# A float32 two-block transformer kernel: the split parts of each feed-forward are placed 32 to 96 bytes further on in SBUF

## The chip, the cores and the metric

The kernel runs on one core of one Trainium2 chip. The metric is the device time of one execution in microseconds (us), lower is better. Three runs of the kernel before took 1274.98, 1275.31 and 1278.06 us; their median is 1275.31 us.

## The reference, cut to what matters

256 tokens of width 1024 go through one block (feed-forward, mixer, feed-forward) and a second, modulated block (mixer, feed-forward). All of it is float32. The part that the change touches is the feed-forward, which comes three times; the third has a small convolution over tokens between the up projection and the product:

```python
D_MODEL, SEQ, D_FF = 1024, 256, 2816
def swiglu(x, w_gate, w_up, w_down):
    return (jax.nn.silu(x @ w_gate) * (x @ w_up)) @ w_down
```

## The kernel before, in words

**Tiles and order.** All weights come from DRAM as one stream of tiles of 128 x 1024 float32 (512 KB) in the order in which they are used. SyncE issues one DMA per tile into a ring of six places (`ring`); the DMA of tile t waits until TensorE has used tile t - 6. Every feed-forward k (0, 1, 2) takes 66 tiles: 22 gate, 22 up, 22 down, in the order down f - 2, gate f, up f.

**The split products.** TensorE multiplies in the type float32r. To keep the precision of float32, each operand is split: the upper part is a copy rounded to float32r, the lower part is the value less the upper part. A product is then three matmuls (`split_product`, L606 to L611):

```python
pe.matmul(out, w_hi[:, cols_], x_hi, start=start, stop=False, **kw)
pe.matmul(out, w_hi[:, cols_], x_lo, start=False, stop=False, **kw)
return pe.matmul(out, w_lo[:, cols_], x_hi, start=False, stop=stop, **kw)
```

Each matmul has a weight load of its own (128 x 128), which runs while the matmul before it still streams its moving operand (128 x 256, the 256 tokens). A tile has 8 chunks of 128 columns, so it makes 24 matmuls, and a feed-forward makes 66 x 24 = 1584: 44 gate and up tiles with 1056 matmuls (`gate_up`, L670, and `gate_up_first`, L688), and 22 down tiles with 528 (`down`, L699). In the gate and up products the moving operand is `u_hi` or `u_lo` (the split input, 8 chunks of 256), in the down products `hidden_hi` or `hidden_lo` (2 chunks of 256, by parity of f). The weights come from `ring_hi` and `ring_lo`.

**Who makes the parts.** ScalarE copies each arrived tile into `ring_hi` (L1429) and each `hidden` into `hidden_hi` (L1435). VectorE subtracts for `ring_lo` (L2074) and `hidden_lo` (L2080); of the tiles from the ninth on, every third `ring_lo` is made by GpSimd instead (L2794). The split inputs `u_hi` and `u_lo` are made once per feed-forward by ScalarE (L1416 and L1997) and VectorE (L2086 and L2092). Between them VectorE takes products (L2143, L2148; in the third feed-forward the convolution, L2160) and, in the first two, adds up the modulation of the second block (`condition`, L2105) in the three places `cond_sums`, which TensorE reads later (L743). All this goes beside TensorE; semaphores count tiles.

**Where things lie.** SBUF is laid out by hand, counted in float32 elements per partition from one start (`regions`, L175). Of these places, each begins 0 or 16 elements past a multiple of 32 elements, which is 0 or 64 bytes past a multiple of 128 bytes:

| name | used for | first element | bytes past a multiple of 128 |
|---|---|---|---|
| `own_parts` (the ring) | lower weights outside the feed-forwards | 0 | 0 |
| `u_parts` | mixer inputs | 8192 | 0 |
| `scratch_parts` | mixer inputs | 16688 | 64 |
| `parts` | all split parts of the feed-forwards; upper weights in the mixers | 20784 | 64 |
| `late_parts` | mixer inputs | 47920 | 64 |
| `branch_parts`, `branch_uppers` | branch inputs and upper weights | 41280, 35136 | 0, 0 |
| `single_upper`, number 18, 19, 20 | upper weights | 47424, 43328, 44352 | 0 |

Inside `parts` lie `ring_hi`, `ring_lo`, `u_hi`, `u_lo`, `hidden_hi` and `hidden_lo` at elements 0, 6144, 12288, 14336, 16384 and 16896 (`PARTS`, L210). Those, and every chunk of 128, 256 or 1024 elements in them, are whole multiples of 128 bytes apart. The same split products are also used in the mixers (`split_cols`, L588), with the operands of the table above.

## Time and profile before

| what | value |
|---|---|
| median of three runs | 1275.31 us (1274.98 to 1278.06) |
| profiled execution, first to last instruction | 1275.3 us |
| mean granted TensorE clock | 0.978 |
| TensorE matmuls, busy | 1215.8 us (95%), 9052 records |
| VectorE / ScalarE / GpSimd, busy | 837.7 / 632.1 / 534.4 us |
| feed-forward matmuls, three groups of 1584 | L609, L610, L611, operands all in `parts` |
| DMA | 207.03 MB, mean 162 GB/s |

The profiled execution's own time is that of its span, 1275.3 us, and is the same as the median of the runs. Matmul records overlap: one is listed with 0.28 us from its start to its end, but the next begins long before that end. What a matmul costs in a stream is the distance from one start to the next. In a view by stretches, a stretch whose ends are put just behind the start of one matmul and of a later one counts the matmuls that start in it and two or three that were still under way when it began; the notes to the rows say which.

### The profile page before, as it was taken

The numbers are of one execution on the slowest core, as the hardware profiler recorded it, in microseconds if no ns is written. First come the engines' busy times: TensorE is split into PE (matmuls) and PEld (weight loads), VectorE is DVE, ScalarE is ACT, GpSimd is POOL, SyncE is SP. The second block draws the span as 40 slices with busy tenths as digits, with TensorE's granted clock in tenths as the row PEclk, the third lists the DMA queues.
The fourth block names the chain that finished last, engine by engine and source line by source line (L and its number), as shares of the span: only waits on it lengthen the run. The fifth ranks groups of instructions, "written<-read, shape, count | busy, mean of one in ns | idle before, by whom it ended". The sixth has DMA issues, their size and how long they took to land.

```text
span 1275.3 us, 24245 instructions
## 1 busy us (share of the span) xinstructions
PE 1215.8 (95%) x9052; PEld 1137.3 (89%) x9052; DVE 837.7 (66%) x1146; ACT 632.1 (50%) x1008; POOL 534.4 (42%) x283
## 2 busy tenths in 40 slices
PE   6999998998999999999999999998899898999998
PEld 6999998976888999999999888977677798999998
DVE  6888875865964577776555843688737685655555
ACT  5444445616651554444435545566417535555553
POOL 0354336632451534334535644478430473232331
PEclk9999998999999999999989999999999998999999
DMA  8677863433333457777504323233212254555553
GB/s 318 234 262 283 281 216 104 149 116 117 116 100 118 163 199 248 279 278 266 181 32 149 125 90 133 84 100 99 83 67 100 83 165 133 185 181 183 186 182 105
DMA packets 58095, 207.03 MB, mean 162 GB/s; under 512 B 6576, under 2 KB 8240, under 8 KB 57776
## 3 DMA queue, kind: packets, MB, share of 16 engines
q1 hardware_dynamic: 49824, 177.23, 40.6%
q0 software_dynamic: 6912, 25.17, 5.4%
q10 hardware_dynamic: 1296, 3.74, 0.8%
q8 instruction: 45, 0.74, 0.2%
q14 instruction: 18, 0.15, 0.0%
HBM read 205.07 MB, written 1.05 MB: 162 GB/s over the span
## 4 chain that ended last, share of the span: by engine, by line
PE 79%; DVE 8%; ACT 4%; issue 4%; POOL 3%; DMA 1%; DVEq 0%; SPq 0%; POOLq 0%; ACTq 0%
PE psum L609 22%; PE psum L610 21%; PE psum L611 21%; PE psum L949 2%; POOL own_parts L2786 2%; PE psum L620 1%; POOL high L2869 1%; PE psum L622 1%; PE psum L621 1%; DMA low<-stream 1%; PE psum L743 1%; DVE parts L2074 1%; PE psum L897 1%; PE psum L663 1%; PE psum L634 1%
## 5 line engine op out<-in xcount | busy, mean ns | idle before, releaser
L609 PE MATMUL psum<-parts 128*128 128x256 f32 x1584 | 452.1, 285 | 17.3 <-DVE parts L2074 9.9
L610 PE MATMUL psum<-parts 128*128 128x256 f32 x1584 | 450.7, 285 | 0.0
L611 PE MATMUL psum<-parts 128*128 128x256 f32 x1584 | 450.6, 284 | 0.0
L609 PEld LDWEIGHTS psum<-parts 128*128 128x128 f32 x1584 | 306.8, 194 | 18.5 <-issue 15.7
L2794 POOL TENSOR_TENSOR parts<-low,parts 128x1024 fp32r<-128x1024 f32 x60 | 158.4, 2640 | 362.4 <-ACT parts L1429 362.4
L610 PEld LDWEIGHTS psum<-parts 128*128 128x128 f32 x1584 | 306.9, 194 | 0.0
L611 PEld LDWEIGHTS psum<-parts 128*128 128x128 f32 x1584 | 306.6, 194 | 0.0
L1429 ACT ACTIVATE parts<-low 128x1024 fp32r<-128x1024 f32 x198 | 207.9, 1056 | 177.8 <-DMA low<-stream 177.0
L2786 POOL TENSOR_TENSOR own_parts<-low,parts 128x1024 fp32r<-128x1024 f32 x76 | 188.0, 2487 | 197.3 <-ACT parts L1498 197.1
L2074 DVE TENSOR_TENSOR parts<-low,parts 128x1024 fp32r<-128x1024 f32 x138 | 164.8, 1218 | 23.3 <-ACT parts L1429 22.0
L611 PE MATMUL psum<-scratch_parts,own_parts 128*128 128x256 f32 (+1 forms) x496 | 150.2, 303 | 0.0
L2786 POOL TENSOR_TENSOR own_parts<-low,single_upper 128x1024 fp32r<-128x1024 f32 x31 | 77.3, 2500 | 73.3 <-ACT single_upper L1498 70.6
L609 PE MATMUL psum<-u_parts,parts 128*128 128x256 f32 x344 | 100.1, 291 | 5.9 <-DVE late_parts L2214 3.1
L611 PE MATMUL psum<-u_parts,own_parts 128*128 128x256 f32 x360 | 101.8, 283 | 0.0
L611 PEld LDWEIGHTS psum<-scratch_parts,own_parts 128*128 128x128 f32 x496 | 96.3, 194 | 3.6
L610 PE MATMUL psum<-late_parts,parts 128*128 128x256 f32 x344 | 97.5, 284 | 0.0
L1498 ACT ACTIVATE parts<-low 128x1024 fp32r<-128x1024 f32 x76 | 79.3, 1050 | 14.3 <-DMA low<-stream 14.2
L609 PE MATMUL psum<-scratch_parts,single_upper 128*128 128x256 f32 (+1 forms) x256 | 79.5, 310 | 6.8 <-POOL own_parts L2786 5.6
L2080 DVE TENSOR_TENSOR parts<-low,parts 128x256 fp32r<-128x256 f32 x66 | 61.2, 927 | 32.0 <-ACT parts L1435 32.0
L2105 DVE SCALAR_TENSOR_TENSOR high<-high,low 128x1024 f32<-128x1024 f32 x64 | 79.0, 1273 | 0.0
L609 PE MATMUL psum<-scratch_parts,parts 128*128 128x256 f32 (+1 forms) x240 | 75.8, 316 | 0.9 <-DVE high L2432 0.6
L609 PEld LDWEIGHTS psum<-u_parts,parts 128*128 128x128 f32 x344 | 66.5, 193 | 11.2 <-issue 7.8
(355 smaller groups left out, 2198.2 us busy)
## 6 DMA issues: line engine op xcount, KB each, us to landing
low<-stream SPq DMA_DIRECT2D x334, 512.0 KB, 3.5
high<-conditioning POOLq DMA_DIRECT2D x48, 512.0 KB, 5.1
high<-wuq ACTq DMA_DIRECT2D x1, 1152.0 KB, 11.0
low<-x SPq DMA_DIRECT2D x4, 256.0 KB, 5.8
high<-ctx ACTq DMA_DIRECT2D x1, 1024.0 KB, 5.7
out<-low SPq DMA_DIRECT2D x8, 128.0 KB, 1.8
low<-cst ACTq DMA_DIRECT2D x1, 850.5 KB, 5.4
low<-vec ACTq DMA_DIRECT2D x1, 157.5 KB, 5.8
```

What stands on the lines that cost most here:

```text
L609: pe.matmul(out, w_hi[:, cols_], x_hi, start=start, stop=False, **kw)
L610: pe.matmul(out, w_hi[:, cols_], x_lo, start=False, stop=False, **kw)
L611: return pe.matmul(out, w_lo[:, cols_], x_hi, start=False, stop=stop, **kw)
L620: pe.matmul(out, hi(k, n), w_hi[:, cols_], start=k == 0, stop=False)
L949: mm = pe.matmul(bank(name)[:, s * T:(s + 1) * T], w[:, (n % 2 * 4 + k) * P:(n % 2 * 4 + k + 1) * P], o[:, k, :], start=k == 0, stop=k == 3)
L1429: act.activation(ring_hi[:, j % RING, :], ring[:, t % RING, :], ACT.Copy)\
L1498: act.activation(weight_place(t), ring[:, t % RING, :], ACT.Copy)\
L2074: dve.tensor_tensor(ring_lo[:, j % RING, :], ring[:, t % RING, :], ring_hi[:, j % RING, :], ALU.subtract).then_inc(S("lower_ready"), 1)
L2080: dve.tensor_tensor(hidden_lo[:, par, :], hidden[:, par, :], hidden_hi[:, par, :], ALU.subtract).then_inc(S("hidden_split"), 1)
L2105: dve.scalar_tensor_tensor(out=acc_, in0=cond_places[g], scalar=small[:, bass.ds(i * 2 + who, 1)], in1=acc_, op0=ALU.mult, op1=ALU.add).th ...
L2786: pool.tensor_tensor(tile_lo[:, t % RING, :], ring[:, t % RING, :], weight_place(t), ALU.subtract).then_inc(S("weights_split"), 1)
L2794: pool.tensor_tensor(ring_lo[:, j % RING, :], ring[:, t % RING, :], ring_hi[:, j % RING, :], ALU.subtract).then_inc(S("lower_ready_2"), 1)
```

## The change

Each of the five regions behind `ring_hi` gets 32 more elements (128 bytes) of room, and a feed-forward reads and writes its parts at a start of its own inside these regions. `PART_STARTS` lists, for each of the three feed-forwards, how many elements further on a part begins: 8, 16 or 24 elements are 32, 64 or 96 bytes; a part that isn't listed begins at 0. The regions' own first elements stay multiples of 32 elements apart, so the bytes past a multiple of 128 become:

| part | feed-forward 0 | 1 | 2 | before |
|---|---|---|---|---|
| `ring_hi` | 64 | 64 | 64 | 64 |
| `ring_lo` | 64 | 0 | 64 | 64 |
| `u_hi` | 0 | 64 | 96 | 64 |
| `u_lo` | 0 | 0 | 96 | 64 |
| `hidden_hi` | 64 | 0 | 96 | 64 |
| `hidden_lo` | 0 | 0 | 32 | 64 |

The whole area grows by 160 elements, so `COND_SUMS` and `COND_PLACES[0]` behind it lie 160 elements further on, and the three `cond_sums` change places among themselves. No instruction, semaphore or wait is added, removed or moved.

```diff
-PARTS, END_PARTS = regions([("ring_hi", RING * TILE), ("ring_lo", RING * TILE), ("u_hi", DC * T), ("u_lo", DC * T),
-                            ("hidden_hi", 2 * T), ("hidden_lo", 2 * T)], 0)
+SHIFT = 32
+PARTS, END_PARTS = regions([("ring_hi", RING * TILE), ("ring_lo", RING * TILE + SHIFT), ("u_hi", DC * T + SHIFT),
+                            ("u_lo", DC * T + SHIFT), ("hidden_hi", 2 * T + SHIFT), ("hidden_lo", 2 * T + SHIFT)], 0)
+PART_STARTS = ({"u_hi": 16, "u_lo": 16, "hidden_lo": 16},
+               {"ring_lo": 16, "u_lo": 16, "hidden_hi": 16, "hidden_lo": 16},
+               {"u_hi": 8, "u_lo": 8, "hidden_hi": 8, "hidden_lo": 24})
...
-        cond_sums = [place(COND_SUMS + g * TILE, TILE) for g in range(3)]
+        cond_sums = [place(COND_SUMS + (g + 1) % 3 * TILE, TILE) for g in range(3)]
...
-        ring_hi, ring_lo, u_hi, u_lo, hidden_hi, hidden_lo = (
-            parts[:, a:a + width].rearrange("p (a b) -> p a b", a=n)
-            for (a, width), n in zip(PARTS.values(), (RING, RING, DC, DC, 2, 2)))
+        def ffn_parts(name, n, width):
+
+            return [parts[:, PARTS[name][0] + starts.get(name, 0):PARTS[name][0] + starts.get(name, 0) + n * width]
+                    .rearrange("p (a b) -> p a b", a=n) for starts in PART_STARTS]
+
+        ring_hi = parts[:, 0:RING * TILE].rearrange("p (a b) -> p a b", a=RING)
+        ring_lo = ffn_parts("ring_lo", RING, TILE)
+        u_hi, u_lo = ffn_parts("u_hi", DC, T), ffn_parts("u_lo", DC, T)
+        hidden_hi, hidden_lo = ffn_parts("hidden_hi", 2, T), ffn_parts("hidden_lo", 2, T)
...
-                return ring_hi[:, j % RING, :], ring_lo[:, j % RING, :]
+                return ring_hi[:, j % RING, :], ring_lo[k][:, j % RING, :]
...
-                                           (hidden_hi[:, par, :], hidden_lo[:, par, :]),
+                                           (hidden_hi[k][:, par, :], hidden_lo[k][:, par, :]),
```

The rest of the diff puts the same index `[k]` at every place where ScalarE, VectorE, GpSimd or TensorE names one of these parts.

## Rows read from the trace of the kernel before

**Rows 1.** The page: busy time of each engine, and the chain that ended last.
```profile
PE 1215.8 (95%) x9052; PEld 1137.3 (89%) x9052; DVE 837.7 (66%) x1146; ACT 632.1 (50%) x1008; POOL 534.4 (42%) x283
...
PE 79%; DVE 8%; ACT 4%; issue 4%; POOL 3%; DMA 1%; DVEq 0%; SPq 0%; POOLq 0%; ACTq 0%
PE psum L609 22%; PE psum L610 21%; PE psum L611 21%; PE psum L949 2%; POOL own_parts L2786 2%; PE psum L620 1%; POOL high L2869 1%; PE psum L622 1%; PE psum L621 1%; DMA low<-stream 1%; PE psum L743 1%; DVE parts L2074 1%; PE psum L897 1%; PE psum L663 1%; PE psum L634 1%
```

**Rows 2.** The page, costliest groups: the feed-forward matmuls and what TensorE waited for.
```profile
L609 PE MATMUL psum<-parts 128*128 128x256 f32 x1584 | 452.1, 285 | 17.3 <-DVE parts L2074 9.9
L610 PE MATMUL psum<-parts 128*128 128x256 f32 x1584 | 450.7, 285 | 0.0
```

**Rows 3.** Stretches inside the three feed-forwards: busy us (x records), clock, DMA share, GB/s.
```profile
core 0: us, PE busy (x), PEclk, DMA share, GB/s
36.00:205.00 169.00, 169.00 (x1411) 1.00 0.71 246
460.50:635.50 175.00, 175.00 (x1461) 1.00 0.69 244
1083.00:1266.00 183.00, 183.00 (x1527) 1.00 0.51 172
```

**Rows 4.** Same view, stretches of split products in the mixers, three records under way at first.
```profile
1015.58:1045.57 29.99, 29.99 (x253) 1.00 0.55 183
219.11:227.05 7.94, 7.94 (x71) 1.00 0.24 76
1053.10:1069.79 16.69, 16.69 (x146) 1.00 0.64 207
659.38:680.12 20.74, 20.74 (x179) 1.00 0.01 2
801.81:804.40 2.59, 2.59 (x25) 1.00 0.52 188
1049.30:1052.97 3.67, 3.67 (x34) 1.00 0.00 0
```

**Rows 5.** TensorE in order of time, three places: start us, us, line, names.
```profile
218.95 0.31 PE L611 MATMUL psum<-u_parts,own_parts 128*128 128x256 f32 x1
219.10 0.28 PE L609 MATMUL psum<-u_parts,parts 128*128 128x256 f32 x1
219.22 0.28 PE L610 MATMUL psum<-late_parts,parts 128*128 128x256 f32 x1
...
801.80 0.28 PE L610 MATMUL psum<-u_parts,single_upper 128*128 128x256 f32 x1
801.92 0.28 PE L611 MATMUL psum<-scratch_parts,own_parts 128*128 128x256 f32 x1
802.03 0.28 PE L609 MATMUL psum<-scratch_parts,single_upper 128*128 128x256 f32 x1
...
1052.84 0.28 PE L610 MATMUL psum<-late_parts,branch_uppers 128*128 128x256 f32 x1
1052.96 0.28 PE L611 MATMUL psum<-u_parts,own_parts 128*128 128x256 f32 x1
1053.08 0.28 PE L609 MATMUL psum<-u_parts,parts 128*128 128x256 f32 x1
```

**Rows 6.** Weight loads in order of time, under matmuls of one column.
```profile
245.89 0.86 PEld L743 LDWEIGHTS psum<-low,high 128*128 128x128 f32 x7
```

**Rows 7.** Stretches of 100 us in each feed-forward, all engines.
```profile
core 0: us, PE busy (x) PEld busy (x) DVE busy (x) ACT busy (x) POOL busy (x), PEclk, DMA share, GB/s
50.00:150.00 100.00, 100.00 (x835) 100.00 (x835) 83.13 (x87) 44.99 (x57) 43.63 (x28) 1.00 0.77 270
470.00:570.00 100.00, 100.00 (x836) 100.00 (x835) 72.21 (x84) 47.05 (x65) 37.52 (x27) 1.00 0.74 263
1100.00:1200.00 100.00, 100.00 (x836) 100.00 (x835) 56.65 (x94) 53.22 (x82) 29.19 (x12) 1.00 0.54 181
```

**Rows 8.** What TensorE waited for in the whole span: us in total, times, longest.
```profile
PE psum L609 <- DVE parts L2074: 9.9, 1, 9.9
PE psum L609 <- POOL own_parts L2786: 7.3, 6, 1.8
PE psum L609 <- DVE parts L2080: 4.9, 4, 1.7
```

**Rows 9.** ScalarE's tile copies into places of either kind: min/median/max ns.
```profile
L1498 ACT ACTIVATE parts<-low x76: 1039/1047/1083, 195.1 to 1061.5; 128x1024 fp32r<-128x1024 f32 x76
L1498 ACT ACTIVATE single_upper<-low x36: 1045/1052/1085, 775.6 to 983.6; 128x1024 fp32r<-128x1024 f32 x36
```

More of the change, by code:

```diff
@@ L1430, in upper, with upper_hidden @@
                    .then_inc(S("upper_ready"), 1)
-            def upper_hidden(par, count):
+            def upper_hidden(k, par, count):
                 act.wait_ge(S("hidden_ready"), count + 1)
-                act.activation(hidden_hi[:, par, :], hidden[:, par, :], ACT.Copy)\
+                act.activation(hidden_hi[k][:, par, :], hidden[:, par, :], ACT.Copy)\
                    .then_inc(S("hidden_upper"), 1)
@@ L2073, in lower, with lower_hidden @@
                 dve.wait_ge(S("upper_ready"), more * RING + (3 * FC * k + j + 1))
-                dve.tensor_tensor(ring_lo[:, j % RING, :], ring[:, t % RING, :], ring_hi[:, j % RING, :],
+                dve.tensor_tensor(ring_lo[k][:, j % RING, :], ring[:, t % RING, :], ring_hi[:, j % RING, :],
                                   ALU.subtract).then_inc(S("lower_ready"), 1)
-            def lower_hidden(par, count):
+            def lower_hidden(k, par, count):
                 dve.wait_ge(S("hidden_upper"), count + 1)
-                dve.tensor_tensor(hidden_lo[:, par, :], hidden[:, par, :], hidden_hi[:, par, :],
+                dve.tensor_tensor(hidden_lo[k][:, par, :], hidden[:, par, :], hidden_hi[k][:, par, :],
                                   ALU.subtract).then_inc(S("hidden_split"), 1)
@@ L2085, in lower_input @@
                 dve.wait_ge(S("input_upper"), DC * k + n + 1)
[L2086 removed]
+                dve.scalar_tensor_tensor(out=u_lo[k][:, n, :], in0=h[:, n, :], scalar=v(g, n), in1=u_hi[k][:, n, :],
                                          op0=ALU.mult, op1=ALU.subtract).then_inc(S("input_split"), 1)
```

27 lines of the change are left out of this document (13 added, 14 removed).

## The prediction

> **What bounds the kernel now.** I read the page first: busy times, then the chain that ended last. TensorE is busy for 1215.8 of 1275.3 us, and 64 of the chain's 100 parts are the three lines of the split product, L609 to L611 [rows 1]. The feed-forwards make 3 x 1584 = 4752 of these matmuls [rows 2]. Then I took the stretches, to see what one costs there. Of the records in each, two or three were still under way at its start; without them the distance from start to start is 169.0/1409 = 119.9 ns, 175.0/1458 = 120.0 ns and 183.0/1525 = 120.0 ns [rows 3], with the clock granted in full (1.00, the 2.4 GHz level). 4752 x 120 ns = 570 us, 45% of the span. It is one value in three stages that differ otherwise: VectorE is busy for 83, 72 and 57% and the DMA share is 0.77, 0.74 and 0.54 [rows 7]. Of all waits of TensorE on the makers of feed-forward parts the list has 9.9 + 4.9 us [rows 8], 9.9 of it once, at the start. So a feed-forward ends 1584 times the distance after it begins, and the question is whether the distance depends on where the operands lie.
>
> **What the mixers show about places.** The same three matmuls run there on other buffers. I call the bytes past a multiple of 128 (the table of places) the phase, and write the four operands as x_hi, x_lo, w_hi, w_lo. Distances, each after three records under way are taken off [rows 4]; the operands' names are in [rows 5]:
> - all four equal (feed-forwards, 64 64 64 64): 120.0 ns. All four 0 (branch products, four other buffers, at 1015 us): 29.99/250 = 120.0 ns.
> - 0 64 64 0 (`u_parts`, `late_parts`, `parts`, `own_parts`): 7.94/68 = 116.8 ns at 219 us, 16.69/143 = 116.7 ns at 1053 us.
> - 64 0 64 0 (`scratch_parts`, `u_parts`, `parts`, `own_parts`): 20.74/176 = 117.8 ns.
> - 64 0 0 0 (upper weight in a `single_upper`): 2.59/22 = 117.7 ns.
> - 0 64 0 0 (upper weight in `branch_uppers`): 3.67/31 = 118.4 ns.
>
> The cleanest pair is inside one stage: at 1052.96 us the upper weights move from `branch_uppers` to `parts` and nothing else changes [rows 5], and the distance goes from 118.4 to 116.7 ns. DMA traffic doesn't sort these stretches: 117.8 ns stands at a share of 0.01 and 120.0 ns at 0.55 [rows 4]. My reading is that a matmul's moving operand and the weight load beside it get into each other's way in SBUF, most of all when everything starts at the same phase. The feed-forwards are at that worst value.
>
> **The rule that speaks against it.** By the Trainium skill (SBUF — State Buffer, "Who interferes with whom") TensorE has one read port for the moving operand and an independent one for the weight load, and waits on nobody. By that rule a place could cost nothing and the sum would be zero; the rows above differ by 3.3 ns without another cause that I can see, so I follow them and keep the rule as a rival.
>
> **The change, part by part.** It moves addresses only. TensorE's terms, matmuls x (120.0 less the distance of the row of the same phases):
> 1. Feed-forward 0, down: phases 64 0 64 64. Both values turned over this is 0 64 0 0, the 118.4 row: 528 x 1.6 = 0.8 us.
> 2. Feed-forward 1, gate and up: 64 0 64 0, the 117.8 row: 1056 x 2.2 = 2.3 us.
> 3. Feed-forward 1, down: 0 0 64 0. No row. Its x_hi differs from w_hi, and x_lo equals w_lo, as in 64 0 0 0: 117.7 ns, 528 x 2.3 = 1.2 us.
> 4. Feed-forward 0, gate and up: 0 0 64 64. No row. Every moving operand differs in phase from the weight loaded beside it, which only 0 64 64 0 has too: 116.7 ns, 1056 x 3.3 = 3.5 us.
> 5. Feed-forward 2: 96 96 64 64, and 96 32 64 64 in the down products. No row has a step of 32 bytes. Every pair differs, so I take 116.7 ns here as well: 1584 x 3.3 = 5.2 us.
>
> Sum 13.0 us. The bounds of terms 4 and 5, which have no row of their own: from above, no gain (120.0 ns). From below, the fastest stream of weight loads: seven loads under one-column matmuls in 0.86 us, less the 0.19 us that one is listed with, over six: 112 ns [rows 6]. As each matmul needs its own load, I take the distance not to go below that: term 4 is then 1056 x 8 = 8.4 us, term 5 1584 x 8 = 12.7 us. I take 116.7, as it is the row that is nearest in kind.
>
> Other engines. ScalarE's tile copies take 1047 ns into `parts` (phase 64) and 1052 ns into a place of phase 0 [rows 9]; 64 bytes do nothing to them that counts. For 32 bytes, and for VectorE and GpSimd, there is no row; all this work lies beside TensorE. If TensorE's distance falls by 3.3 ns, a turn of six tiles shrinks by 6 x 24 x 3.3 = 475 ns, and VectorE's share in feed-forward 0 goes from 83 to 86% [rows 7]. The tightest chain is the one over `hidden`: three tiles are between the last up product and the down that needs it, 72 x 3.3 = 0.24 us less. TensorE waited for L2080 four times for 4.9 us in all [rows 8]; were each 0.24 us longer, that would be 1 us, and most would stay as they are. I count 0.3 us against. The `cond_sums` that change places are read and written by the same instructions as before, beside TensorE: zero; with their cover gone they would still take the same time, as only addresses change.
>
> The sum: 1275.3 - 13.0 + 0.3 = 1262.6 us, say 1262.5. The profiled execution's own time is the 1275.3 us of its span, and the median of the runs is 1275.31, so nothing has to be added.
>
> **The rivals.**
> - *Deeper (chance 0.2).* With one phase for both inputs and one for both weights, terms 4 and 5 settle near the floor of the loads. For: the distance is that steady in feed-forwards (one value over 1400 matmuls), so a good phase would be as steady as the bad one. Against: no mixed stretch has a mean below 116.7. Time: 1275.3 - 0.8 - 2.3 - 1.2 - 8.4 - 12.7 = 1249.9 us; less, if VectorE then holds `hidden` back (72 x 8 = 0.6 us less room).
> - *Nothing (0.12).* What sorts the stretches isn't the place but the buffers (one tensor against several), or the ports are as independent as the skill says. For: that page. Against: the branch products, with three buffers, run at 120.0. Time: 1275.3 us. That the parts don't really move is excluded: the new starts are in the addresses of reader and writer alike.
> - *Slower (0.08).* A start that is 32 bytes off the 64-byte raster, which no split operand has today, makes the moving read touch one piece more (17 in place of 16 of 64 bytes): an estimate of 120 x 17/16 = 127.5 ns, for the 1584 matmuls of feed-forward 2: +11.9 us. Terms 1 to 4 bring 7.8, so this would be 1279.4 us. It decides from 124.9 ns in feed-forward 2 upwards, where it eats up the rest.
> - The forecast has 0.6. Its own range, with term 5 between nothing and twice its size, is 1257 to 1268 us.
>
> **How the numbers follow.** 0.3% (3.8 us) is about what a measurement of this kernel tells from no change. The forecast and the deeper case are faster by more than that, 0.8; of the case of nothing, a fifth could still be a small gain; the slower case straddles the bound. So faster 0.82, same 0.11, slower 0.07. The range is to leave out no more than 2 in 10: it takes in the forecast, the deeper case with some of feed-forwards 0 and 1 below their rows (1246), and reaches up to the edge of the case of nothing (1274).
>
> **What would show it.** In the changed profile, the same three stretches, taken with their counts: about 117.2 ns in feed-forward 0 on average over gate, up and down, 117.8 in feed-forward 1, and whatever the 32 bytes give in feed-forward 2. The mixer stretches must stay at 116.7 to 120.0 ns, as no address there moves. Feed-forward 1 is the test of the reading, as both its phases stand nearly in rows: if it stays at 120.0 while its phases are those of the 117.8 row, the reading is wrong. The forecast fails by size if feed-forward 2 is not near 116.7, and by kind if TensorE's waits for L2074, L2080 or L2794 grow by more than 1 us.

## The result, and the profile after

Over 20 runs each, the changed kernel takes 1269.59 us (1264.12 to 1280.01) where the kernel before takes 1277.84 us (1273.52 to 1284.38). The ratio is 0.9944 [0.9928, 0.9961]: 0.56% or 7.2 us faster, with 5.0 to 9.2 us as its interval (the two medians are 8.3 us apart, the two means 7.4). The forecast was 12.8 us under the median then known. The sign and the wide range (1246 to 1274 us) held; the size did not, and 1269.59 us is also outside the 1257 to 1268 us that the prediction gave its own case.

One thing about the base. The profiled execution of before has a span of 1275.3 us, but an execution's own time is 1.7 to 1.9 us above its span in every run on record (after: 1264.12 against 1262.3). So the base of the sum should have been 1277.0 us, not 1275.3: that the median of three was the same number is chance.

The page of the kernel after, its engines, chain and feed-forward groups (all lines of the kernel stand 12 further down: L621 is L609, L2086 is L2074, L2092 is L2080, L2798 is L2786, L2806 is L2794):

```profile
PE 1201.9 (95%) x9052; PEld 1124.2 (89%) x9052; DVE 836.1 (66%) x1146; ACT 631.7 (50%) x1008; POOL 525.8 (42%) x283
...
PE 78%; DVE 7%; issue 4%; ACT 4%; POOL 4%; DMA 2%; DVEq 0%; POOLq 0%; SPq 0%; ACTq 0%
...
L621 PE MATMUL psum<-parts 128*128 128x256 f32 x1584 | 448.0, 283 | 18.2 <-DVE parts L2086 10.3
```

TensorE is 13.9 us less busy than before [rows 1], with the same number of records; GpSimd is 8.6 us less busy, VectorE and ScalarE and the shape of the chain stayed. Where it went is in the stretches of the three feed-forwards. The columns are start:end, length, PE busy (records), granted clock, DMA share and GB/s:

```profile
36.66:202.56 165.90, 165.90 (x1414) 1.00 0.74 252
457.78:629.05 171.27, 171.27 (x1462) 1.00 0.72 250
1071.81:1253.62 181.81, 181.81 (x1540) 1.00 0.54 173
```

Three matmuls were under way at each start, so the distance is 165.90/1411 = 117.6, 171.27/1459 = 117.4 and 181.81/1537 = 118.3 ns, where all three had 120.0 [rows 3]. Within the first two feed-forwards the gate and up products can be told from the down products, since a tile of each has its own operands. The same view, one or two tiles of each kind, and last the branch products of the mixer, of which no address moved:

```profile
53.12:55.81 2.69, 2.69 (x26) 1.00 0.91 294
55.93:61.47 5.54, 5.54 (x50) 1.00 0.65 194
460.10:465.64 5.54, 5.54 (x50) 1.00 0.52 148
465.75:468.44 2.69, 2.69 (x26) 1.00 0.63 207
1006.37:1036.36 29.99, 29.99 (x253) 1.00 0.56 186
```

These read 2.69/23 = 117.0 ns (down, feed-forward 0), 5.54/47 = 117.9 (gate and up, 0), 117.9 (gate and up, 1), 117.0 (down, 1) and 29.99/250 = 120.0 ns. The mixer stayed at its value of before [rows 4] to the hundredth of a microsecond, and so did the other kinds of mixer products (116.8, 117.8 and 118.4 ns in both traces), so the change of distance follows the moved operands alone. Over all records of a kind the means are 117.05, 117.88, 117.83, 116.53 and, in feed-forward 2, 118.3 for both.

Last, what TensorE waited for in the whole span (total, times, longest):

```profile
PE psum L621 <- DVE parts L2086: 10.3, 1, 10.3
PE psum L621 <- POOL own_parts L2798: 8.7, 7, 2.5
PE psum L621 <- DVE parts L2092: 5.7, 5, 1.6
```

Against [rows 8] these grew by 0.4, 1.4 and 0.8 us. The first and the last are feed-forward waits; the middle one belongs to the mixers, and in the second profile of this kernel (e8_after_again) it is 7.2 us, as before.

The sizes add up in this way. By its five terms the distances are worth 10.6 us (below). From first to last matmul the feed-forwards shrank by 3.4, 2.7 and 3.2 us, 9.3 in all; in e8_after_again by 7.7. Two things took the difference. One is waits and other long distances at the full clock level: in all three feed-forwards together they are 0.5 us (after) and 0.6 us (e8_after_again) more than before. The other is the clock. Stretches of feed-forward matmuls at half the clock, in the kernel after and in e8_after_again:

```profile
441.10:446.70 5.60, 5.60 (x27) 0.50 0.01 3
37.40:40.70 3.30, 3.30 (x18) 0.51 0.05 14
```

At this level (1.2 GHz) the distance is 213 ns with the operands of before and with those of the changed kernel alike, so the layout brings nothing there and each such matmul costs over 90 ns more. The three feed-forwards of before have 39 of them, those of after 45 and those of e8_after_again 62, most of them just behind the start of feed-forwards 1 and 2. Against before that is 0.6 and 2.2 us.

The other 3.7 of the 13.0 us between the two spans are outside the feed-forwards and are no effect of the change that I can show. The mean granted clock was 0.978 before and 0.982 after, which is 58.3 and 46.4 us at the 1.2 GHz level by the traces' clock records (49.9 and 36.6 us of it outside the feed-forwards); in the changed kernels of this study it was 46 to 66 us. A microsecond at that level costs a stream of matmuls about 0.44 us (213 against 120 ns), so 13 us less of it can account for the 3.7. Over the 20 runs of the changed kernel the time rises by 1.5 us for each 0.001 that the mean granted clock is lower (correlation -0.80): the clock goes with most of the 16 us between the fastest and the slowest run.

### The profile page after: what moved, and what is told of

It is laid out like the page before. It is cut to its first block, busy times and chain, and to the rows that moved or that the text cites. A ratio compares the mean times of both kernels' runs of the same rounds, so it can differ in the third digit from the quotient of the medians.

```text
span 1262.3 us, 24245 instructions
## 1 busy us (share of the span) xinstructions
PE 1201.9 (95%) x9052; PEld 1124.2 (89%) x9052; DVE 836.1 (66%) x1146; ACT 631.7 (50%) x1008; POOL 525.8 (42%) x283
## 4 chain that ended last, share of the span: by engine, by line
PE 78%; DVE 7%; issue 4%; ACT 4%; POOL 4%; DMA 2%; DVEq 0%; POOLq 0%; SPq 0%; ACTq 0%
PE psum L621 22%; PE psum L622 21%; PE psum L623 21%; POOL own_parts L2798 2%; PE psum L961 2%; POOL high L2881 2%; PE psum L632 1%; PE psum L633 1%; PE psum L634 1%; DMA low<-stream 1%; PE psum L755 1%; PE psum L646 1%; DVE parts L2086 1%; PE psum L909 1%; PE psum L936 1%
## 5 line engine op out<-in xcount | busy, mean ns | idle before, releaser
L621 PE MATMUL psum<-parts 128*128 128x256 f32 x1584 | 448.0, 283 | 18.2 <-DVE parts L2086 10.3
L622 PE MATMUL psum<-parts 128*128 128x256 f32 x1584 | 446.7, 282 | 0.0
L623 PE MATMUL psum<-parts 128*128 128x256 f32 x1584 | 445.3, 281 | 0.0
L621 PEld LDWEIGHTS psum<-parts 128*128 128x128 f32 x1584 | 300.2, 190 | 19.5 <-issue 16.8
L623 PEld LDWEIGHTS psum<-parts 128*128 128x128 f32 x1584 | 301.5, 190 | 0.0
L622 PEld LDWEIGHTS psum<-parts 128*128 128x128 f32 x1584 | 301.4, 190 | 0.0
L2806 POOL TENSOR_TENSOR parts<-low,parts 128x1024 fp32r<-128x1024 f32 x60 | 150.4, 2506 | 361.4 <-ACT parts L1441 361.4
L1441 ACT ACTIVATE parts<-low 128x1024 fp32r<-128x1024 f32 x198 | 207.9, 1056 | 177.6 <-DMA low<-stream 172.9
L2798 POOL TENSOR_TENSOR own_parts<-low,parts 128x1024 fp32r<-128x1024 f32 x76 | 187.7, 2483 | 195.7 <-ACT parts L1510 195.5
L2086 DVE TENSOR_TENSOR parts<-low,parts 128x1024 fp32r<-128x1024 f32 x138 | 164.4, 1218 | 23.8 <-ACT parts L1441 22.9
L2798 POOL TENSOR_TENSOR own_parts<-low,single_upper 128x1024 fp32r<-128x1024 f32 x31 | 77.1, 2492 | 72.0 <-ACT single_upper L1510 69.3
L621 PE MATMUL psum<-u_parts,parts 128*128 128x256 f32 x344 | 100.0, 291 | 5.9 <-DVE late_parts L2226 3.1
L621 PE MATMUL psum<-scratch_parts,single_upper 128*128 128x256 f32 (+1 forms) x256 | 79.7, 311 | 8.2 <-POOL own_parts L2798 7.0
L1510 ACT ACTIVATE parts<-low 128x1024 fp32r<-128x1024 f32 x76 | 79.3, 1051 | 14.0 <-DMA low<-stream 13.9
L2092 DVE TENSOR_TENSOR parts<-low,parts 128x256 fp32r<-128x256 f32 x66 | 62.1, 940 | 32.0 <-ACT parts L1447 32.0
L622 PE MATMUL psum<-u_parts,single_upper 128*128 128x256 f32 (+1 forms) x256 | 76.3, 298 | 0.0
L621 PEld LDWEIGHTS psum<-u_parts,parts 128*128 128x128 f32 x344 | 66.3, 193 | 11.1 <-issue 7.7
```

The source lines that it names most:

```text
L1441: act.activation(ring_hi[:, j % RING, :], ring[:, t % RING, :], ACT.Copy)\
L1510: act.activation(weight_place(t), ring[:, t % RING, :], ACT.Copy)\
L2086: dve.tensor_tensor(ring_lo[k][:, j % RING, :], ring[:, t % RING, :], ring_hi[:, j % RING, :], ALU.subtract).then_inc(S("lower_ready"), 1)
L2092: dve.tensor_tensor(hidden_lo[k][:, par, :], hidden[:, par, :], hidden_hi[k][:, par, :], ALU.subtract).then_inc(S("hidden_split"), 1)
L2798: pool.tensor_tensor(tile_lo[:, t % RING, :], ring[:, t % RING, :], weight_place(t), ALU.subtract).then_inc(S("weights_split"), 1)
L2806: pool.tensor_tensor(ring_lo[k][:, j % RING, :], ring[:, t % RING, :], ring_hi[:, j % RING, :], ALU.subtract).then_inc(S("lower_ready_2"), 1)
```

## The experiments

Offsets below are in bytes. A layout is written as three numbers: how far x_hi, x_lo and w_lo start past w_hi, **modulo 256**. That unit is a result of the experiments, and the expectations quoted were written while it was still in dispute. In these terms the kernel before has 0 0 0 everywhere, and the changed one has

| products | layout (x_hi, x_lo, w_lo) | distance in the kernel, ns |
|---|---|---|
| feed-forward 0, gate and up | 192 64 0 | 117.9 |
| feed-forward 0, down | 128 64 0 | 117.0 |
| feed-forward 1, gate and up | 128 64 64 | 117.8 |
| feed-forward 1, down | 192 64 64 | 116.5 |
| feed-forward 2, gate and up | 160 32 0 | 118.3 |
| feed-forward 2, down | 160 96 0 | 118.3 |

### Streams with nothing beside them

The first experiment is TensorE alone: 164 streams of 48 float32r matmuls of the kernel's shape, each with its own weight load, in the order of the kernel's products. All of the reference's computation is left out, and so are the weights' DMAs and the work of the other engines. Only the starts differ between streams.

```diff
+STREAMS = [
+    ('one', 0, 0, 0, 0),
+    ('one', 1, 0, 0, 0),
...
+    ('gate', 0, 0, 0, 0),
+    ('gate', 0, 0, 0, 8),
...
+    ('down', 24, 24, 0, 24),
...
+                pe.matmul(out, w_hi, x_hi, start=first, stop=False, skip_group_check=True)
+                pe.matmul(out, w_hi, x_lo, start=False, stop=False, skip_group_check=True)
+                return pe.matmul(out, w_lo, x_hi, start=False, stop=last, skip_group_check=True)
```

> This kernel leaves out the whole computation and keeps only TensorE: 164 streams of 48 float32r matmuls each (128x128 weights, 256 columns), every stream with other starts, in elements of 4 bytes past the places that the changed kernel uses; nothing else runs beside them. First 32 streams with one start for all inputs (0 to 124 bytes in steps of 4) and one for all weights, then all 64 combinations of 0, 32, 64, 96 bytes for upper input, lower input and lower weight, once in the pattern of gate and up, once in that of down. Theory A (the read of the moving operand collides with the weight load under it, by their phase modulo 128 bytes): 120.0 ns from start to start where all phases are equal, the same 117.9 / 117.1 / 117.9 / 116.6 / 118.3 ns as in the changed kernel's feed-forwards for their patterns, and no difference whether all are moved together. Theory B (what is in the way are the other engines' and the DMA's accesses to SBUF, at phases that fit the old layout): with nothing beside it every stream has the same distance, at most 117 ns. Theory C (the steps between parts, not the phases, decide): distances differ from those of the kernel for the same phases by more than 1 ns.

The regions of this kernel begin where those of the changed kernel do, so its smallest start of an input is 128 modulo 256. Stretches of one stream each, with 44 distances (47 records less the three under way). First three layouts: one start for all inputs at 144; then the order of the gate products at 128 0 0, and at 128 0 64:

```profile
47.38:52.37 4.99, 4.99 (x47) 1.00 0.02 3
230.26:235.51 5.25, 5.25 (x47) 1.00 0.01 3
241.75:246.88 5.13, 5.13 (x47) 1.00 0.00 0
```

That is 113.4, 119.3 and 116.6 ns, with a DMA share of 0.02 or less and no other engine at work. So the place alone decides over 6 ns of 119. Then two streams that read the same inputs, from the same start, and one set of weights each; in the second the weights start 64 bytes further on:

```profile
70.06:75.22 5.16, 5.16 (x47) 1.00 0.00 0
224.50:229.78 5.28, 5.28 (x47) 1.00 0.00 0
```

117.3 ns with the inputs 160 bytes past the weights and 120.0 with them 96 past. In this run and in the second streams run the value goes with the difference of the two starts and not with either of them: 96 bytes gives 120.0 from both weight starts, 64 bytes 117.8. So the read of the inputs and the load of the weights do affect each other.

The streams with the starts of the changed kernel gave 117.8, 116.8, 117.8, 115.7 and 118.3 ns in the order of the table, against 117.9, 117.0, 117.8, 116.5 and 118.3 in the kernel: the streams stand for the kernel to about 1 ns. Theory B, the other engines and the DMA, falls: with nothing beside TensorE most streams stay above its 117 ns. The order of gate and of down products made no difference (0.2 ns). Steps of 4 bytes, off the 16-byte raster, gave 117.6 to 123.2 ns, and only there did this kernel pass 120 (123.2 ns at 132 bytes, 121.1 at 136).

By the Trainium skill (SBUF — State Buffer, "Who interferes with whom") TensorE's two read ports are independent and it never waits on anyone. With TensorE alone on the chip the distance still depends on the starts, from 113 to 123 ns. Read as "a place costs nothing", as the rival in the prediction read it, the rule doesn't hold for this kind of stream, and the measurement decides; whether it is at the ports that the two reads meet is not shown.

### The layouts passed on

The changed kernel with its three sets of starts given to other feed-forwards:

```diff
-PART_STARTS = ({"u_hi": 16, "u_lo": 16, "hidden_lo": 16},
-               {"ring_lo": 16, "u_lo": 16, "hidden_hi": 16, "hidden_lo": 16},
-               {"u_hi": 8, "u_lo": 8, "hidden_hi": 8, "hidden_lo": 24})
+PART_STARTS = ({"u_hi": 8, "u_lo": 8, "hidden_hi": 8, "hidden_lo": 24},
+               {"u_hi": 16, "u_lo": 16, "hidden_lo": 16},
+               {"ring_lo": 16, "u_lo": 16, "hidden_hi": 16, "hidden_lo": 16})
```

> The changed kernel with its three layouts passed on by one: feed-forward 0 has the layout of 2, 1 that of 0, 2 that of 1. Theory A: the distances go with the layout: 118.3 ns in feed-forward 0, 117.9 (gate, up) and 117.1 (down) in feed-forward 1, 117.9 and 116.6 in feed-forward 2; the sum stays, about 10.5 us below 4752 x 120 ns. Rival (each layout fits its own feed-forward, by what runs beside it there): at least one layout gives 119 ns or more in its new place, and the three feed-forwards together become over 3 us longer than in the changed kernel.

```profile
37.29:138.72 101.43, 101.43 (x862) 1.00 0.78 262
460.57:631.99 171.42, 171.42 (x1462) 1.00 0.73 249
1077.67:1257.32 179.65, 179.65 (x1533) 1.00 0.54 175
```

Feed-forward 0 now has the 118.1 ns (101.43/859) that feed-forward 2 had, and 1 and 2 have 117.5 and 117.4. Each value went with its layout and not with the stage. The three feed-forwards together took 1.9 us more than in the changed kernel, less than the rival's 3 us; feed-forward 0 took 195.0 us, hardly less than before, as more waits in it took back what the distance gave. The time was 1267.78 us against 1276.57 in one run each.

### One operand moved at a time

Feed-forward 0 moves the lower inputs only, 1 the upper inputs only, 2 the lower weights only (beside the 128 bytes that the wider regions bring):

```diff
+PART_STARTS = ({"u_lo": 16, "hidden_lo": 16},
+               {"u_hi": 16, "hidden_hi": 16},
+               {"ring_lo": 16})
```

> One kind of part moved by 64 bytes in each feed-forward, the others at 0: 0 only the lower inputs, 1 only the upper inputs, 2 only the lower weights. Theory A in its strict form (only the pair of moving operand and the weight load under it counts): lower inputs alone free one matmul in three, about 118.9 ns (a third of the 3.3 ns); upper inputs alone free two in three, about 117.8 ns; lower weights alone free one in three, about 118.9 ns. Rival (it matters whether one read starts at another phase than the read before it on the same port, so every change of phase counts): all three at 117 to 118 ns, lower weights alone too.

```profile
36.39:201.53 165.14, 165.14 (x1414) 1.00 0.73 252
456.24:628.07 171.83, 171.83 (x1462) 1.00 0.73 249
1076.24:1257.62 181.38, 181.38 (x1543) 1.00 0.54 174
```

117.0, 117.8 and 117.8 ns, at 1268.03 us against 1276.57 in one run each. That is the rival's outcome and not the thirds of theory A: in the prediction's unit, one operand moved brings as much as two or three. The feed-forward with only its lower inputs moved is faster than the one that the prediction gave its best value for having "every pair different". That criterion, which terms 4 and 5 stood on, falls here in the unit in which it was stated. (Modulo 256 the upper inputs of feed-forwards 0 and 2 are 128 bytes away as well, so two operands differ there; e6_by_128 below tests the criterion in that unit.)

### The unit, and the best places

Streams alone again (all of the computation left out), 223 of them, over 512 bytes and with steps of 16:

```diff
+    ('one', 28, 0, 0, 0),
...
+    ('gate', 4, 4, 0, 0),
...
+    ('gate', 48, 48, 0, 0),
...
+    ('gate', 0, 32, 0, 0),
```

> Again only TensorE's streams of 48 matmuls, the rest of the computation left out; now the six regions begin at the same place modulo 256 bytes, and starts go over 256 bytes (one address pattern for all: over 512). In the first streams kernel one input start and one weight start for all three matmuls gave 113.3 ns at 64 bytes (192 bytes modulo 256, as the input region began 128 bytes past), while upper and lower input each 64 bytes on, the lower weight in its own region, gave 117.8 ns at the same phases modulo 128. Theory D (the distance repeats every 256 bytes, and there the two input regions were 128 bytes apart): upper and lower input both at 192 bytes give 113.3 ns with the lower weight in its own region; both at 144 too; all three equal give 120.0 ns constant, as in the kernel before; one address pattern for all repeats after 256 bytes. Theory E (it repeats every 128 bytes, and 113.3 comes from reading the same weights and inputs three times): upper and lower input at 192 bytes stay at 117.8 ns, and one address pattern for all repeats after 128 bytes. Theory F (no address rule: the rhythm depends on what ran before): the four streams with all operands equal, each behind another stream, differ among themselves by more than 1 ns.

Stretches of the streams with all inputs at 112 bytes, and at 368; then 16 16 0, and 0 128 0:

```profile
111.01:115.99 4.98, 4.98 (x47) 1.00 0.00 0
201.58:206.56 4.98, 4.98 (x47) 1.00 0.00 0
252.25:257.24 4.99, 4.99 (x47) 1.00 0.00 0
382.40:387.54 5.14, 5.14 (x47) 1.00 0.00 0
```

The first two are the same 4.98/44 = 113.2 ns, and the whole row of starts repeats after 256 bytes (0 and 256 both give 120.0; 112, 192, 368 and 448 give 113.3 to 113.4). 16 16 0 gives 113.4. The last, 116.8 ns, moves one operand by 128 bytes, which is nothing by the prediction's unit, and gives nearly half of the possible gain. The mixers' rows of the prediction have the streams' values too when they are counted modulo 256: 64 0 64 has 116.7 there and 116.8 here, 0 64 64 117.8 and 117.8, 192 0 0 117.7 and 117.8. Repeats of 0 0 0 agreed within 0.3 ns (119.7 to 120.0). One thing did not fit: 16 16 0 had 118.7 ns near the start of this run and 113.4 here, and all inputs at 144 had 118.8, where the first experiment had 113.4.

Steps of 128 bytes and nothing else were then put into the kernel:

```diff
+SHIFT = 64
+PARTS, END_PARTS = regions([("ring_hi", RING * TILE), ("ring_lo", RING * TILE), ("u_hi", DC * T + SHIFT),
+                            ("u_lo", DC * T + SHIFT), ("hidden_hi", 2 * T + SHIFT), ("hidden_lo", 2 * T + 48)], 0)
...
+PART_STARTS = ({"u_hi": 32, "u_lo": 32, "hidden_hi": 32, "hidden_lo": 32},
+               {"u_hi": 32, "hidden_hi": 32},
+               {"u_lo": 32, "hidden_lo": 32})
```

> Only steps of 128 bytes, so that every phase modulo 128 is that of the kernel before: feed-forward 0 upper and lower inputs, 1 only upper inputs, 2 only lower inputs. Theory A as I predicted with it (phases modulo 128 bytes): 120.0 ns in all three, 1277 us. Theory D (modulo 256 bytes, the streams' values): 118.7, 119.8 and 116.8 ns, so the last feed-forward is 5.1 us shorter and the kernel is at about 1270 us.

```profile
36.81:204.25 167.44, 167.44 (x1414) 1.00 0.72 249
459.40:634.48 175.08, 175.08 (x1462) 1.00 0.71 244
1080.17:1260.60 180.43, 180.43 (x1535) 1.00 0.54 175
```

118.7 ns with both inputs at 128, 120.0 with x_hi alone, 117.8 with x_lo alone. Modulo 128 all three are the kernel before, and should all be 120.0. The unit of the prediction is wrong, and the 128 bytes that each wider region adds are a part of the change. The criterion of different pairs falls in the new unit too: with both inputs moved every input starts elsewhere than the weights and the distance is 118.7 ns, with x_lo alone two of three matmuls keep an equal pair and it is 117.8. The third value missed the stream's 116.8 by 1 ns, the second clue. The time was 1271.05 us in one run.

The three best starts of the streams, one for each feed-forward (same regions as above):

```diff
+PART_STARTS = ({"u_hi": 4, "u_lo": 4, "hidden_hi": 4, "hidden_lo": 4},
+               {"u_hi": 28, "u_lo": 28, "hidden_hi": 28, "hidden_lo": 28},
+               {"u_hi": 48, "u_lo": 48, "hidden_hi": 48, "hidden_lo": 48})
```

> The changed kernel with regions that begin at the same place modulo 256 bytes and, for upper and lower inputs alike (hidden ones too), starts of 16 bytes in feed-forward 0, 112 in feed-forward 1 and 192 in feed-forward 2; the lower weights stay at 0. These are the three starts at which TensorE's streams alone took 113.3 ns. Theory D (the address rule modulo 256 bytes holds in the kernel too): 113.3 ns in each feed-forward, so each is 1584 x 6.7 = 10.6 us shorter than before the change, the kernel about 1277 - 32 = 1245 us. Rival (beside ScalarE's, VectorE's and GpSimd's work and the DMAs the rhythm of 113.3 ns breaks): 116 ns or more in at least one of them, and a kernel at 1255 us or above.

```profile
36.50:201.12 164.62, 164.62 (x1414) 1.00 0.74 254
456.73:622.10 165.37, 165.37 (x1462) 1.00 0.74 258
1070.74:1252.12 181.38, 181.38 (x1543) 1.00 0.53 174
```

Only feed-forward 1 (112 bytes) has the value of its stream, 165.37/1459 = 113.3 ns. The others have 116.7 (16 bytes) and 117.8 (192 bytes) where the streams had 113.3. The time was 1262.54 us in one run, 13.8 less than the median of 1276.38 of before on this chip.

### Several rhythms for one layout

To see whether this is the stage's doing, all three feed-forwards got 16 bytes:

```diff
+PART_STARTS = ({"u_hi": 4, "u_lo": 4, "hidden_hi": 4, "hidden_lo": 4},
+               {"u_hi": 4, "u_lo": 4, "hidden_hi": 4, "hidden_lo": 4},
+               {"u_hi": 4, "u_lo": 4, "hidden_hi": 4, "hidden_lo": 4})
```

> All upper and lower inputs of all three feed-forwards start 16 bytes past a multiple of 256 bytes counted from the weights' starts, the lower weights at 0. Theory D: 113.3 ns, 4752 x 6.7 = 31.8 us less than before the change (ratio 0.975), and 0.981 of the changed kernel. Rival: what TensorE gains is taken back by waits for the hidden parts (VectorE) in feed-forwards 0 and 1, where it is busiest: ratio above 0.980 with waits of over 3 us more on L2092's equivalent.

Stretches of feed-forward 0, then two inside feed-forward 1:

```profile
36.64:204.08 167.44, 167.44 (x1414) 1.00 0.72 249
511.35:570.57 59.22, 59.22 (x502) 1.00 0.78 268
581.17:633.79 52.62, 52.62 (x454) 1.00 0.66 223
```

118.7, then 59.22/499 = 118.7, then 52.62/451 = 116.7 ns: within one feed-forward, with the same addresses, the distance changes. Between the two stretches TensorE had short waits for `hidden_lo`. In feed-forward 0 the 67 distances before the stretch shown, between two waits, had a fourth value, 8.04/67 = 120.0 ns. Feed-forward 2 had 116.7 throughout, and 113.3 came nowhere. The median of 9 runs was 1270.29 us, ratio 0.9940 [0.9912, 0.9968]: no better than the change.

The changed kernel was run again beside it, to see whether its values hold:

> The changed kernel itself once more, for times on the same chip as the others. From its own trace the three feed-forwards together are 9.3 us shorter than before: ratio 0.9927. If part of the 13.0 us of its profiled execution was chance in the granted clock (46.4 us at half clock against 58.3 us), the ratio lies at 0.992 to 0.995; if the whole 13.0 us belong to the change, at 0.990.

They did: 117.86 and 116.54 ns in feed-forward 1, 117.88 and 117.03 in 0, and 118.3 in 2, each within 0.03 ns of the first profile. Its six runs have a median of 1267.0 us, ratio 0.9926 [0.9898, 0.9954].

Then TensorE alone (all of the computation left out), ten layouts, each entered twelve times after a wait for a ScalarE copy of another width:

```diff
+    if PAUSES[s]:
+        mm.then_inc(sems["asked"], 1)
+        pe.wait_ge(sems["paused"], sum(1 for v in PAUSES[:s] if v) + 1)
```

> TensorE's streams alone again, the rest of the computation left out: ten layouts (upper input, lower input, lower weight in bytes modulo 256 past the upper weight: 0 0 0; 16 16 0; 112 112 0; 192 192 0; 192 64 0; 128 64 0; 128 64 64; 160 32 0; 64 64 128; 0 128 0), each in twelve streams of 48 matmuls, and ahead of each stream TensorE waits for a ScalarE copy of another length (64 to 768 columns). Theory G (a layout allows several rhythms, and the moment at which TensorE starts again after a wait picks one, which then holds until the next wait): within one layout the streams take different constant distances, such as 113.3, 116.7 and 118.7 ns for 16 16 0, as the three feed-forwards of the kernel with 16 bytes everywhere did. Theory D alone (the layout sets one distance): all twelve streams of a layout within 0.3 ns.

Three successive entries of 16 16 0, then two of 192 192 0:

```profile
111.12:116.34 5.22, 5.22 (x47) 1.00 0.00 0
117.44:122.42 4.98, 4.98 (x47) 1.00 0.00 0
123.56:128.69 5.13, 5.13 (x47) 1.00 0.01 3
...
270.68:275.86 5.18, 5.18 (x47) 1.00 0.00 0
283.16:288.15 4.99, 4.99 (x47) 1.00 0.00 0
```

118.6, 113.2 and 116.6 ns from the same instructions on the same addresses; then 117.7 and 113.4. These are the values that the kernels had shown for those layouts. Over all entries:

| layout | distances at its entries, ns |
|---|---|
| 0 0 0 (the kernel before) | 119.9 to 120.0, always |
| 112 112 0 | 113.9 to 114.2, always |
| 192 64 0, and 128 64 64 | 117.8 to 117.9, always |
| 160 32 0 | 118.3 to 118.4, always |
| 128 64 0 | 118.75 once, else 116.8 to 117.0 |
| 0 128 0 | 117.7 to 117.9 (116.8 in the streams before) |
| 192 192 0 | 117.8 twice, then 113.3 to 113.7 ten times |
| 64 64 128 | 118.8 and 113.6 in turn |
| 16 16 0 | 118.6 or 118.7 five times, 116.8 five times, 113.3 twice |

A layout allows one steady distance or several. Where there are several, the restart after a wait picks one, and the stream keeps it until the next wait; in the feed-forwards of the kernels here it changed only behind a single distance of 135 ns or more, apart from some settling in the first two dozen matmuls. (In the streams of the first two experiments a change of layout without a wait picked one as well.) The four of the changed kernel's six layouts in the table have one each, but for one entry of 128 64 0.

The picks were tested once more in the kernel, with the three starts of before turned round:

```diff
+PART_STARTS = ({"u_hi": 48, "u_lo": 48, "hidden_hi": 48, "hidden_lo": 48},
+               {"u_hi": 4, "u_lo": 4, "hidden_hi": 4, "hidden_lo": 4},
+               {"u_hi": 28, "u_lo": 28, "hidden_hi": 28, "hidden_lo": 28})
```

> The three starts of the kernel with three layouts, each in another feed-forward: 192 bytes in 0, 16 in 1, 112 in 2. Distances then were 116.7 (16 bytes, in 0), 113.4 (112, in 1) and 117.8 ns (192, in 2). If a layout sets its distance: 117.8, 116.7, 113.4 ns. Theory G: at least one of the three differs from its former value by more than 1 ns.

Feed-forward 0 in two stretches (192 bytes), then feed-forward 1 in two (16 bytes):

```profile
36.57:177.32 140.75, 140.75 (x1198) 1.00 0.76 263
181.95:203.14 21.19, 21.19 (x190) 1.00 0.57 186
458.39:550.20 91.81, 91.81 (x790) 1.00 0.74 255
550.95:630.10 79.15, 79.15 (x670) 1.00 0.71 243
```

117.8 and, after short waits, 113.3 ns; 116.7 and, after a single distance of 164 ns, too short for the profile to list as a wait, 118.7 ns. Feed-forward 2, now at 112 bytes, had 113.3. The time was 1265.06 us, once, against a median of 1278.72 of before.

### The place that always gives the fast distance

All three feed-forwards at 112 bytes:

```diff
+PART_STARTS = ({"u_hi": 28, "u_lo": 28, "hidden_hi": 28, "hidden_lo": 28},
+               {"u_hi": 28, "u_lo": 28, "hidden_hi": 28, "hidden_lo": 28},
+               {"u_hi": 28, "u_lo": 28, "hidden_hi": 28, "hidden_lo": 28})
```

> Inputs of all three feed-forwards 112 bytes past the weights modulo 256, the lower weights at 0. In the kernel with three layouts this one held 113.4 ns through feed-forward 1. If it falls into that rhythm from any start: 113.4 ns in all three, 4752 x 6.6 = 31 us less than before, ratio 0.976. Theory G: at least one feed-forward (0 and 2 begin after other waits) settles in another rhythm of 116 ns or more, ratio 0.980 to 0.995.

```profile
36.23:60.16 23.93, 23.93 (x214) 1.00 0.63 210
462.30:543.36 81.06, 81.06 (x718) 1.00 0.75 256
1072.70:1247.01 174.31, 174.31 (x1541) 1.00 0.56 181
```

113.4, 113.4 and 113.3 ns. The time is 1258.81 us (five runs, 1257.55 to 1261.4) against 1278.72 us (nine runs): ratio 0.9851 [0.9834, 0.9869], 19.1 us faster, and the best version of the study. So the expectation was right in its distances and missed in its ratio, which fell where theory G had put it for another reason: 4752 x 6.6 ns would be 31 us. From first to last matmul, feed-forwards 1 and 2 shrank by 6.4 and 10.9 us, and feed-forward 0 by 0.5: it took 195.2 us, against 195.7 before. What TensorE waited for, over feed-forward 0 (10 to 205.5 us):

```profile
PE psum L621 <- DVE parts L2092: 5.9, 10, 1.6
```

Ten waits for `hidden_lo` where the changed kernel had two there. VectorE's subtractions for `ring_lo` in feed-forward 0, here and in the kernel before (min/median/max ns), then two of them on VectorE and the GpSimd subtraction beside them (start, length, engine, line, operation, tile, records):

```profile
L2086 DVE TENSOR_TENSOR parts<-low,parts x45: 1210/1219/3468, 12.2 to 191.1; 128x1024 fp32r<-128x1024 f32 x45
L2074 DVE TENSOR_TENSOR parts<-low,parts x45: 1208/1214/1227, 12.2 to 190.5; 128x1024 fp32r<-128x1024 f32 x45
...
63.15 4.59 DVE L2086 TENSOR_TENSOR parts<-low,parts 128x1024 fp32r<-128x1024 f32 x2
```

```profile
62.46 3.06 POOL L2806 TENSOR_TENSOR parts<-low,parts 128x1024 fp32r<-128x1024 f32 x1 [0.84 <-ACT parts L1441]
```

Two of L2086 took 2.35 us in the kernel before. Here the first begins inside a GpSimd subtraction, and the pair loses 4.59 - 2.35 = 2.24 us, about what was left of that subtraction (62.46 + 3.06 - 63.15 = 2.37 us). Seven of the 45 are long like this, one every 17.5 us or so, each 2.2 us too long, and a TensorE wait for `hidden_lo` follows each within 7 us. In the kernel before none is. The shorter subtraction for `hidden_lo` already met GpSimd there: 20 of its 22 in feed-forward 0 were long (up to 1.57 us, where 0.43 is the least), with only two waits of TensorE. So what is new at the faster pace is that the `ring_lo` subtraction falls behind GpSimd's as well. The Trainium skill (SBUF — State Buffer, "Who interferes with whom") says that a VectorE instruction with two inputs in SBUF contends with a GpSimd instruction that reads SBUF. The trace agrees: products that take one input from PSUM (L2148 in the kernel before) begin inside GpSimd subtractions too and take 0.42 us each time. No run here took the GpSimd work away to show it.

So VectorE should be what bounds feed-forward 0. The last run takes work from it: the sums of the modulation (`condition`) are made over 64 of 1024 columns in feed-forward 0, which leaves the rest of the second block's modulation out.

```diff
-                            dve.scalar_tensor_tensor(out=acc_, in0=cond_places[g], scalar=small[:, bass.ds(i * 2 + who, 1)],
-                                                     in1=acc_, op0=ALU.mult, op1=ALU.add).then_inc(S("cond_steps"), 1)
+                            n_ = 64 if k == 0 else TILE
+                            dve.scalar_tensor_tensor(out=acc_[:, 0:n_], in0=cond_places[g][:, 0:n_],
+                                                     scalar=small[:, bass.ds(i * 2 + who, 1)], in1=acc_[:, 0:n_],
+                                                     op0=ALU.mult, op1=ALU.add).then_inc(S("cond_steps"), 1)
```

> The kernel with 112 bytes everywhere, with VectorE relieved in feed-forward 0: of the modulation sums there only the first 64 of 1024 columns are computed, the rest is left out (the modulation of the second block is then not the reference's). With 112 bytes everywhere the distance in feed-forward 0 was 113.4 to 114.1 ns, but it took 195.2 us, as TensorE waited for the lower hidden part 10 times, 5.9 us, and more where the waits are too short for the list. If VectorE's load is what gives the gain back: these waits go, and feed-forward 0 takes 184 to 188 us. Rival (the DMA or GpSimd's lower weights can't keep up with a distance of 113.4 ns): it stays above 192 us.

The stretch of feed-forward 0 that now runs without a break, and the wait for `hidden_lo` in that feed-forward:

```profile
62.23:197.69 135.46, 135.46 (x1198) 1.00 0.78 269
```

```profile
PE psum L621 <- DVE parts L2092: 4.0, 3, 1.9
```

135.46/1195 = 113.4 ns over three quarters of the feed-forward, which took 187.6 us and not 195.2. The whole took 1247.86 us in its one run, against 1280.13. The distance is as good as the streams promise once VectorE keeps up. None of the 45 subtractions of L2086 in feed-forward 0 is long in this run (1228 ns at most), so it doesn't tell VectorE's amount of work from its meetings with GpSimd; the rival, the DMA or GpSimd's pace, is out with 187.6 us against its 192. As work is left out, the time of the whole is not that of a usable kernel.

## Why the prediction was right or wrong

**The mechanism was right.** The distance between these matmuls depends on where their operands start, and on the start of the inputs against that of the weights, as the reading had it. The feed-forwards were at a bad place (of more than a hundred layouts on the 16-byte raster, one was slower by more than 0.2 ns, 192 64 128 with 121.0), and moving them brought the time down. The unmoved mixer products kept their distance. That waits for late operands would take something back was right too: both feed-forward waits of [rows 8] grew, neither by more than 1 us.

**The rule of independent ports**, the case of nothing (0.12), fell. **Slower** (0.08) fell as well: 32 bytes gave 118.3 ns and not 127.5. Starts with a slower value exist, but off the 16-byte raster (up to 123.2 ns), where the change has none. **Deeper** (0.2) had a real price, 113.3 ns, but no stretch of the changed kernel shows it, nor does any entry of the four of its layouts that e9_pauses tried: its condition was one phase for both inputs and one for both weights, and it stood on the wrong unit: 160 32 is one phase modulo 128 and two modulo 256.

**What failed is the size of terms 4 and 5**, and behind it the step that gave them 116.7 ns because every pair of starts is different modulo 128 bytes. The runs showed 117.9 and 118.3 ns, another unit (256 bytes), and no such criterion in either unit. Term by term, matmuls x (120.0 less the measured mean):

| term | forecast, us | measured, us |
|---|---|---|
| 1. feed-forward 0, down | 0.8 | 528 x 2.95 = 1.6 |
| 2. feed-forward 1, gate and up | 2.3 | 1056 x 2.17 = 2.3 |
| 3. feed-forward 1, down | 1.2 | 528 x 3.47 = 1.8 |
| 4. feed-forward 0, gate and up | 3.5 | 1056 x 2.12 = 2.2 |
| 5. feed-forward 2 | 5.2 | 1584 x 1.7 = 2.7 |
| sum | 13.0 | 10.6 |

- Term 5 is the worst. It had no row, and I took 116.7, "nearest in kind", for every pair being different; it was 118.3. With one operand moved, and so with pairs that stay equal modulo 128, a feed-forward ran at 117.0 ns (e3_one_part); modulo 256, every pair different gave 118.7 and two of three pairs equal 117.8 (e6_by_128). The number of different pairs doesn't set the distance.
- Term 4 rests on the same step: 117.9 and not 116.7.
- Terms 1 and 3 were too small by 1.4 us together. The "phase" modulo 128 put them on rows of other layouts: the wider regions also move `u_hi` and `hidden_hi` by 128 bytes, which counts. That term 2 was exact with the same wrong unit is luck. (Modulo 256 the operands of its row, 64 0 64 0, are 0 64 64, another layout than the kernel's 128 64 64; both have 117.8.)
- I read one distance for one layout. A layout can have several, and a short stretch shows whichever its last wait picked. The layout of the `single_upper` row has 117.7 to 118.2 ns in most of its stretches of this trace and 118.9 to 119.4 in three; the row didn't say so.
- The returned time was 0.3 us in the sum. It was 1.3 us in one profile and 2.9 in the other (10.6 less the 9.3 and 7.7 us by which the feed-forwards shrank). Waits took 0.5 and 0.6 us of it, which the sum had about right; the rest is matmuls at the half clock level, a term that the sum didn't have.
- **The base** was 1.7 us too low, from taking the span for the execution's time. Corrected, the forecast would have been 1264.3, at the same distance from before.

10.6 us less 1.3 to 2.9 us is 7.7 to 9.3 us, within or just past the edge of the measured 5.0 to 9.2 us and inside the 5.9 to 13.0 us of e8_after_again's ratio.

**What stays open.** That the start of the inputs against that of the weights decides is shown; where the two reads meet, in the memory, at a port or in TensorE, is not, and a clash in SBUF is only argued. Nor is it shown whether a layout with several rhythms picks the same one in every execution; each kernel has one trace or two.

## What to carry to other kernels

Where float32r matmuls follow each other, each with its own weight load, take the distance from start to start by stage and class; if it is well above 113 ns for 256 columns, try the streamed inputs 112 bytes (modulo 256, on the 16-byte raster) past the weights first. It is tested here for 256 columns and these split products only. Try a layout over several entries after waits and not only once, and prefer one that has a single value over one whose best value is as good. Then look at the engine that makes the operands: here VectorE, held up by GpSimd, took back nearly all of the gain in one of three stages.

## What the runs showed of the hardware

- The distance of these matmuls takes steady values from 113.3 to 121.0 ns at starts on the 16-byte raster, by the relative starts modulo 256 bytes, with the clock granted in full and nothing else running. At the 1.2 GHz level it was 213 ns with either kernel's layouts.
- One layout (16 16 0) ran at 113.3, 116.7, 118.7 or 120.0 ns, chosen at a restart; the 118.7 was kept over more than 1400 matmuls.
- Starts 4 bytes and 8 bytes off the raster, at 132 and 136, cost 123.2 and 121.1 ns.
- A VectorE subtraction of 128 x 1024 with both inputs in SBUF took 3.45 us and not 1.22 when it began inside a GpSimd subtraction; VectorE products with one input in PSUM kept their 0.42 us.
- The time at the half clock level moved between 46 and 66 us in executions of like kernels. As each microsecond of it costs a stream of matmuls about 0.44 us, that can move the total by some 9 us, as much as this change does; the stretches at full clock show the effect where the total time needs 20 runs.
